# One order of the split products in a two-layer encoder: each weight piece's high products first, then its low ones

## The reference

```python
p = h @ w_in_even[e]            # 2048 x 3072, layer 0
mix = concat([y_a, y_b]) @ w_out_even[e]     # 2048 x 2048
p = h @ w_in_odd[o]             # 2048 x 6160, layer 1
mix = att @ w_out_odd[o]        # 2048 x 2048
x = x + mix
up = h @ w_up                   # 2048 x 11264, both layers
x = x + (silu(gate) * val) @ w_down          # 5632 x 2048, both layers
```

## Time and profile before

| | |
|---|---|
| median of 3 runs | 2144.76 us (2144.58 to 2144.89) |
| span of the profiled execution | 2143.7 us |
| TensorE busy | 2118.6 us (99%), 11076 products |
| weight loads busy | 1804.1 us (84%) |
| VectorE busy | 1453.7 us (68%) |
| ScalarE busy | 1043.5 us (49%) |
| DMA | 185 GB/s over the span, 397 MB |

### The profile page before, as it was taken

How to read it: one execution, slowest core, us unless ns; L and a number is a source line. 1 busy time by engine, 2 the same in 40 slices (tenths; PEclk the granted TensorE clock), 3 DMA queues, 4 the chain that set the end, 5 groups by cost and what they waited for, 6 DMA issues and landing times.

```text
span 2143.7 us, 29615 instructions
## 1 busy us (share of the span) xinstructions
PE 2118.6 (99%) x11076; PEld 1804.1 (84%) x11076; DVE 1453.7 (68%) x1587; ACT 1043.5 (49%) x1078; POOL 30.2 (1%) x59
## 2 busy tenths in 40 slices
PE   7999999999999999999999999999999999999997
PEld 6888888888888888887888888888888888888886
DVE  5786486776767767676556555577776677766776
ACT  6554464445444454455444444464444444444453
POOL 0000000000000000000011000000000000000000
PEclk9999999999999999999999999999999999999999
DMA  8655465555555555654565555555555555555552
GB/s 271 194 172 199 163 198 195 190 182 189 183 195 189 183 189 183 196 180 156 186 192 172 184 183 184 178 179 193 195 177 195 178 194 194 178 195 178 195 189 86
DMA packets 317235, 397.18 MB, mean 185 GB/s; under 512 B 8660, under 2 KB 240380, under 8 KB 317052
## 3 DMA queue, kind: packets, MB, share of 16 engines
q1 hardware_dynamic: 313724, 392.06, 55.9%
q0 software_dynamic: 1056, 3.16, 0.7%
q10 hardware_dynamic: 2400, 1.20, 0.2%
HBM read 394.29 MB, written 2.11 MB: 185 GB/s over the span
## 4 chain that ended last, share of the span: by engine, by line
PE 97%; ACT 1%; DVE 1%; issue 0%; DMA 0%; ACTq 0%; DVEq 0%
PE ps_turned L1249 39%; PE ps_turned L1251 20%; PE ps_straight L1266 12%; PE ps_straight L1268 12%; PE ps_straight L1267 12%; ACT w_high L439 1%; PE ps_turned L1288 1%; PE ps_straight L1457 0%; PE ps_straight L1474 0%; DMA x<-in_x 0%; ACT work L459 0%; DVE w_low L796 0%; PE ps_straight L1466 0%; PE ps_straight L1359 0%; PE ps_straight L1485 0%
## 5 line engine op out<-in xcount | busy, mean ns | idle before, releaser
L1249 PE MATMUL ps_turned<-h_split,w_high 128*128 128x512 f32 x3584 | 1270.0, 399 | 0.0
L796 DVE TENSOR_TENSOR w_low<-w_raw,w_high 128x2048 fp32r<-128x2048 f32 x369 | 845.8, 2293 | 314.6 <-ACT w_high L439 270.6
L1251 PE MATMUL ps_turned<-h_split,w_low 128*128 128x256 f32 x3584 | 1006.1, 281 | 0.0
L439 ACT ACTIVATE w_high<-w_raw 128x2048 fp32r<-128x2048 f32 x369 | 707.4, 1919 | 543.8 <-PE ps_straight L1268 313.5
L1249 PEld LDWEIGHTS ps_turned<-h_split,w_high 128*128 128x128 f32 x3584 | 673.4, 188 | 166.6 <-issue 0.2
L1251 PEld LDWEIGHTS ps_turned<-h_split,w_low 128*128 128x128 f32 x3584 | 676.9, 189 | 1.1
L1266 PE MATMUL ps_straight<-w_high,y_split 128*128 128x512 f32 x960 | 375.5, 391 | 0.0
L1268 PE MATMUL ps_straight<-w_high,y_split 128*128 128x512 f32 x960 | 374.0, 390 | 0.0
L1267 PE MATMUL ps_straight<-w_low,y_split 128*128 128x512 f32 x960 | 373.7, 389 | 0.0
L448 ACT ACTIVATE work<-ps_turned 128x512 f32<-128x512 f32 x112 | 67.1, 599 | 323.3 <-PE ps_turned L1251 277.9
L1268 PEld LDWEIGHTS ps_straight<-w_high,y_split 128*128 128x128 f32 x960 | 180.2, 188 | 38.2
(11 more groups left out here) (184 smaller groups left out, 658.2 us busy)
## 6 DMA issues: line engine op xcount, KB each, us to landing
w_raw<-in_w_up SPq DMA_DIRECT2D x176, 1024.0 KB, 5.1
w_raw<-in_w_down SPq DMA_DIRECT2D x88, 1024.0 KB, 5.1
w_raw<-in_w_in_odd SPq DMA_DIRECT2D x48, 1024.0 KB, 5.4
w_raw<-in_w_in_even SPq DMA_DIRECT2D x24, 1024.0 KB, 5.4
w_raw<-in_w_out_even SPq DMA_DIRECT2D x16, 1024.0 KB, 5.0
w_raw<-in_w_out_odd SPq DMA_DIRECT2D x16, 1024.0 KB, 5.0
x<-in_x SPq DMA_DIRECT2D x4, 512.0 KB, 9.3
work<-c_rows POOLq DMA_DIRECT2D x8, 256.0 KB, 4.5
```

The lines of the kernel that those rows point to most:

```text
L439: a.activation(wh[:, s, :], raw[:, s, :], ACT.Copy).then_inc(s_high, 1)
L796: ve.tensor_tensor(wl[:, s, :], raw[:, s, :], wh[:, s, :].bitcast(F32), ALU.subtract).then_inc(s_low, 1)
L1249: pe.matmul(bank, hi[:, kk, P * m:P * m + P], acts[:, K, :], start=(K == 0), stop=False, skip_group_check=True)
L1251: ins = pe.matmul(bank[:, TOK:], lo[:, kk, P * m:P * m + P], acts[:, K, 0:TOK], start=False, stop=(K == KC - 1), skip_group_check=True)
```

## The change

In both kinds of pieces the two kinds of weights are separated. A piece first waits for its high half (`s_high`) and takes all products with high weights, then waits for its low half (`s_low`) and takes all products with low weights. In a turned piece that is 16 products of 512 columns and then 16 of 256, where the two widths alternated. In a straight piece it is 16 products with high weights, high and low activations in turn, and then 8 with low weights. The first token tile is now complete after the 20th of 24 products, where it was after the 12th, and so is `s_tile0`. Products, weight loads, operands and PSUM banks are the same. `pool_product` is left as it is.

```diff
--- before.py
+++ after.py
@@ -1241,15 +1241,18 @@
                 s = c % RING
                 hi = wh[:, s, :].rearrange("p (k n) -> p k n", k=8)
                 lo = wl[:, s, :].rearrange("p (k n) -> p k n", k=8)
+                pe.wait_ge(s_high, at(c + 1, 12, r))
+                for m in range(2):
+                    for kk in range(8):
+                        K = 8 * k + kk
+                        pe.matmul(psT[:, 2 * slot + m, :], hi[:, kk, P * m:P * m + P], acts[:, K, :], start=(K == 0),
+                                  stop=False, skip_group_check=True)
                 pe.wait_ge(s_low, at(c + 1, 12, r))
                 for m in range(2):
-                    bank = psT[:, 2 * slot + m, :]
                     for kk in range(8):
                         K = 8 * k + kk
-                        pe.matmul(bank, hi[:, kk, P * m:P * m + P], acts[:, K, :], start=(K == 0), stop=False,
-                                  skip_group_check=True)
-                        ins = pe.matmul(bank[:, TOK:], lo[:, kk, P * m:P * m + P], acts[:, K, 0:TOK], start=False,
-                                        stop=(K == KC - 1), skip_group_check=True)
+                        ins = pe.matmul(psT[:, 2 * slot + m, TOK:], lo[:, kk, P * m:P * m + P], acts[:, K, 0:TOK],
+                                        start=False, stop=(K == KC - 1), skip_group_check=True)
                 ins.then_inc(s_used, 1)
 
             def straight_quad(c, slot, acts, k0, first, last, r=0, tile0=None):
@@ -1257,15 +1260,20 @@
                 s = c % RING
                 hi = wh[:, s, :].rearrange("p (k n) -> p k n", k=4)
                 lo = wl[:, s, :].rearrange("p (k n) -> p k n", k=4)
+                def product(t, kk, weights, al, begin, end):
+                    a0 = P * t + (TOK if al else 0)
+                    return pe.matmul(psA[:, 2 * slot + t, :], acts[:, k0 + kk, a0:a0 + P], weights[:, kk, :],
+                                     start=begin, stop=end)
+
+                pe.wait_ge(s_high, at(c + 1, 12, r))
+                for t in range(2):
+                    for kk in range(4):
+                        product(t, kk, hi, False, first and kk == 0, False)
+                        product(t, kk, hi, True, False, False)
                 pe.wait_ge(s_low, at(c + 1, 12, r))
                 for t in range(2):
-                    bank = psA[:, 2 * slot + t, :]
                     for kk in range(4):
-                        ah = acts[:, k0 + kk, P * t:P * t + P]
-                        al = acts[:, k0 + kk, TOK + P * t:TOK + P * t + P]
-                        pe.matmul(bank, ah, hi[:, kk, :], start=(first and kk == 0), stop=False)
-                        pe.matmul(bank, ah, lo[:, kk, :], start=False, stop=False)
-                        ins = pe.matmul(bank, al, hi[:, kk, :], start=False, stop=(last and kk == 3))
+                        ins = product(t, kk, lo, False, False, last and kk == 3)
                     if t == 0 and tile0 is not None:
                         ins.then_inc(tile0, 1)
                 ins.then_inc(s_used, 1)
```

## The result

The changed kernel takes 2123.86 us (median of 4 runs, 2121.79 to 2124.71) against 2144.67 us before (4 runs): a ratio of 0.9901, interval 0.9888 to 0.9913, or 20.8 us less. The forecast was 2127.4 us, 17.4 us less.

The account below looks back on a forecast made before the run. TensorE's stream of products was taken to bound the kernel. Turned pieces -15.7, start -1.9 and end +0.2 gave -17.4 us, from 2144.8 to 2127.4 us, with a range of 2100 to 2160.

Parts of the forecast that it names:

- The bound: Whole kernel: TensorE's stream of products sets the time, busy 2118.6 of 2143.7 us; gains come mainly from pace.
- The 512-column half: High-weight half of a turned piece: 11 products at 232.7 ns and 5 at 226.7, 3693 ns.
- The settling: Behind alternating widths, 512-column products need some 11 products at 232.7 ns before the stream runs at 226.7.
- The 256-column half: Low-weight half of a turned piece: 118 ns a product, 115.5 to 120.5; with the other half 70 ns less a piece.
- The argument for 118 ns: Forget-gate sums with 16-column loads also show 0.12 us behind a 256-column product, so the load doesn't set that slot.
- The fourth case: Slower rival: in unbroken runs of 256-column products loads no longer hide, 127.5 ns a slot, 2161 us; chance 0.17.
- The straight pieces: New order in the 144 straight pieces: 226.7 ns a product stays, effect nothing.
- The added wait: 368 more TensorE waits in mid-piece: nothing; a rival gave 73 ns each, 26.9 us, chance 0.04.
- The start: First products wait only for the high half, a second wait goes too: 1.9 us gained, bounds 0 and 3.3.
- The end: Last piece: `s_tile0` fires after the 20th product, so VectorE starts later: 0.2 us lost, bounds 0 and 0.5.
- Launch: About 1.1 us around the profiled span of 2143.7 us, against the median of 2144.76.
- The case "nothing changes": Rival: a pair's cost belongs to its slots and loads, not their order; 2143.1 us, 2138 to 2148; chance 0.18.

Follow-up runs that it names:

- e_order: Kernel before with the new product order in both kinds of pieces, but one wait on the low half at a piece's start: 2125.46 us against 2144.56.
- e_turned: Kernel before with new order and waits in the turned pieces alone, straight pieces as before: 2125.72 us against 2144.56.
- e_hi64: Kernel before, still alternating, with most high-weight products of turned pieces halved to 64-column loads and half the partitions: 2100.94 us against 2144.7.
- e_straight: Kernel before with new order and waits in the straight pieces alone, turned pieces as before: 2143.72 us against 2144.56.
- e_wait: Kernel before in its old order, with separate waits for high and low halves, the low one after a piece's first product: 2144.45 us against 2144.56.
- e_run8: Kernel before with turned pieces in runs of 8 high, then 8 low products, one wait at the start: 2129.84 us against 2144.57.
- e_run4: Kernel before with turned pieces in runs of 4 high, then 4 low products, one wait at the start: 2135.67 us against 2144.7.
- e_snake: Changed kernel with the second piece of each pair taking its low products first, giving runs of 32: 2122.17 us against 2144.57 for the kernel before.
- e_best: e_snake with the last piece tile by tile again and L1343 one piece later: 2117.63 us against 2144.7 for the kernel before.

## Why the prediction was right, step by step

- **The bound.** TensorE's stream sets the time, and the change works through the pace of turned pieces: shown by `e_order` and `e_turned`, each of which has all but a few us of the gain, at the start and the end.
- **The 512-column half.** Predicted 3693 ns from the first 11 products of a straight stretch; measured 3653 as the mean of the three pieces above. The settling is real but smaller: 26 ns, not 66. The row was the nearest, but the stretch before it alternated; behind an unbroken narrow run the stream settles sooner, after five products (233, 236, 228, 232 and 231 ns, then 227).
- **The 256-column half.** Predicted 118 ns a product, measured 119.6, 120 in the long run, inside the 115.5 to 120.5 that the forecast allowed. Taken with the half above: 70 ns a piece forecast, 84 measured, 15.7 against 18.8 us. That is most of the 3.5 us by which the forecast was too high. The wide half was put 40 ns too long and the narrow one 25 ns too short, so it is partly luck that the sum is nearer than its larger term.
- **The argument for 118 ns doesn't carry it.** I took the forget gate's sums as a sign that the load doesn't set the narrow slot. `e_hi64`, with a 64-column load and a product half as large, has 114 ns where full loads have 117, so something of the two does move it. And the same full load gives 117 in alternation and 120 in a long run, so that a slot read in alternation was no measure of one in a run. The number was near, because 109 and 126.5 enclosed it, not for the reason given. The fourth case, that a narrow slot grows in an unbroken run, was right in its direction: it grew by some 2.6 ns, 40 ns a piece, where that case has 127.5 ns. It was outweighed by the wide slots, which became 8 ns shorter.
- **The straight pieces.** Nothing, as predicted: 5.44 us a piece; `e_straight`.
- **The added wait.** Nothing, as predicted; `e_wait`.
- **The start.** Predicted 1.9 us, measured 2.3 between the two profiled executions, but not by its own working. The products reached full pace earlier too, so the lead grew to 5 us; the wait on VectorE at L1343, with the slow products behind it, then took back 2.7. The prediction had such a wait as its lower bound, but not the clock's fall. The 2.3 us themselves are on the high side. In the nine profiled kernels that keep the old first wait (the kernel before among them) the first turned product starts between 66.2 and 67.6, in the three with the new wait and the stall at L1343 between 65.1 and 65.6, on average 1.7 us earlier. The moment at which the pace rises moves too: in the traces' records of the clock the full clock (2.4 GHz) begins at 17.5 to 20.4 us in the nine and at 14.2 to 15.6 in the three. By medians the changed kernel is 1.6 us below `e_order`, and `e_straight` is 0.8 below the kernel before with the end's 0.25 against it. So 1.1 to 2.3 us are what the runs allow.
- **The end.** Predicted 0.2 us, measured 0.25.
- **Launch.** The prediction put 1.1 us around the span. Every later run has 1.7 to 1.8 us, and the kernel before, run beside the experiments, has a span of mostly 2142.4 to 2143.6 us; its profiled execution was one of the longer ones. No step hung on it.

The case "nothing changes", in which a pair costs what it costs in any order, falls with the changed kernel itself and with `e_run8` and `e_run4`: the same pairs take 348, 349 and 351 ns there and 353 ns in alternation. The Trainium skill (TensorE: Matmul & The Clock Gate, "Back-to-back issue gap") gives 109 and 216 ns for the two widths, the estimates cited in the prediction. The lowest averages seen here are 114 and 226.7 ns, 5% more, and nothing tried here brought them lower; why is open.

## What to carry to other kernels

Where short and long products alternate on TensorE, each with a weight load of its own, read the distance from start to start and compare each width's slot with its slot among its like; then try the orders. Here runs of sixteen and more were the fastest, runs of 2 came within 6 ns a piece of sixteen, and runs of 4 were the slowest of the grouped ones, so one length tried says little about the next. A wait split in two is free where what it waits for is long ready, and worth something only where it ends last, here at the first pieces alone. An earlier start is kept only if no later wait takes it back: look at what TensorE meets next, and move that.

## What was not expected of the hardware

- An alternating pair takes 353 ns with full loads, 346 with a half load and half product for the low weights, 341 with them for the high weights, and 346 where both loads are of 16 columns. Most of the difference lies in the wide slot (236, 229, 227 and 229 ns). Why isn't explained, and load length alone doesn't order them.
- A narrow slot isn't a constant under a full load: 117 ns in alternation, 115 in runs of 2, 120 in long runs.
- The cost of short runs isn't monotonic: for a turned piece 5651 ns in alternation, 5573 in runs of 2, 5620 in runs of 4, 5580 in runs of 8, 5567 in runs of 16 and 5555 in runs of 32 (cycles as read above). Runs of 2 don't escape the dear wide slots (233 ns each); they have the shortest narrow ones, and why stays open.
- A wait of 2.1 us at L1343 was followed by 3.3 us at a granted clock of 0.50, and it cost more than its length. The same is in the traces of `e_snake` and `e_straight`, with waits of 2.1 us there; behind the 1.0 us of the kernel before and the 1.3 us of `e_wait` the clock stayed at 1.00. The kernels with the longer wait have runs 2 us and more apart (`e_straight` 2141.3 and 2143.7, the changed kernel 2121.8 and 2123.9, `e_snake` 2119.7 and 2122.5), `e_best` without it stays within 0.5 us. That the shorter ones among them kept the clock was not seen in a profile; for the changed kernel and `e_snake` the mean clock of the run fits it, 0.998 in the shortest and 0.997 in the others, while in `e_straight` three of the longer runs have 0.998 too.
